# PEER expert stage: 112 candidate sums in place of 256, one-hot products on VectorE alone, four U blocks in flight, work between transpose and subtraction

## The reference, cut to what matters

```python
s = jnp.einsum('thpc,hpnc->thpn', q, keys32)
sv, si = lax.top_k(s, PEER_TOPK)                                   # 16 of 128 in each half
cand = (sv[:, :, 0, :, None] + sv[:, :, 1, None, :]).reshape(..., 256)
cidx = (si[:, :, 0, :, None] * N_SUBKEYS + si[:, :, 1, None, :]).reshape(..., 256)
cs, ci = lax.top_k(cand, PEER_TOPK)                                # 16 of the 256 sums
eidx = jnp.take_along_axis(cidx, ci, axis=-1)
g = jax.nn.softmax(cs, axis=-1)
act = jax.nn.gelu(jnp.einsum('thkd,td->thk', U[eidx], xb))
out = jnp.einsum('thk,thkd->td', g * act, V[eidx])
```

## Time and profile before

| what | value |
|---|---|
| time, median of 3 runs | 3904.52 us (3902.64 to 3905.26) |
| profiled execution: its time / its span | 3908.76 us / 3907.0 us |
| PE, DVE, ACT, POOL busy over the span | 87%, 76%, 27%, 29% |
| mean granted TensorE clock | 0.926 |
| moved from and to HBM | 822.80 MB, 211 GB/s |

### The profile page before, as it was taken

One profiled execution on the slowest core, in us unless ns is written; L12 is line 12 of the kernel. 1 busy time (PEld: TensorE's weight loads), 2 busy tenths in 40 slices (PEclk: granted clock), 3 DMA queues, 4 the chain that ended last, 5 costly groups with the idle time before them and its releaser, 6 DMA issues. The chain is left out here.

```text
span 3907.0 us, 52941 instructions
## 1 busy us (share of the span) xinstructions
PE 3384.6 (87%) x17880; PEld 3084.6 (79%) x17880; DVE 2964.2 (76%) x4958; ACT 1063.2 (27%) x1419; POOL 1152.0 (29%) x892
## 2 busy tenths in 40 slices
PE   6997558799799999888888886757999999999978
PEld 6996446699699999888888876756888888888878
DVE  3112773488788887999999987766999899999953
ACT  3213342211122222434343421112222222222233
POOL 0000000000000001666666766652333334333300
PEclk9998668899899999999999988888999999999989
DMA  3223211111234333888888899998999999999821
GB/s 105 91 91 103 78 49 50 27 39 36 77 100 135 99 98 109 278 275 278 276 287 280 281 302 327 314 330 301 355 356 355 340 355 356 355 359 354 297 77 49
DMA packets 411348, 822.80 MB, mean 211 GB/s; under 512 B 40704, under 2 KB 262800, under 8 KB 403856
## 3 DMA queue, kind: packets, MB, share of 16 engines
q1 hardware_dynamic: 300688, 419.27, 32.7%
q0 software_dynamic: 110592, 402.70, 30.2%
HBM read 696.74 MB, written 125.12 MB: 210 GB/s over the span
## 5 line engine op out<-in xcount | busy, mean ns | idle before, releaser
L232 PE MATMUL ea_pa<-rest_hi,ea_uhi 128*128 128x384 f32 x2048 | 738.2, 360 | 166.7 <-DVE ea_ulo L1428 166.7
L233 PE MATMUL ea_pa<-rest_lo,ea_uhi 128*128 128x384 f32 x2048 | 721.7, 352 | 0.0
L234 PE MATMUL ea_pa<-rest_hi,ea_ulo 128*128 128x384 f32 x2048 | 721.2, 352 | 0.0
L1136 POOL DMA_INDIRECT h<-in_peer_u,ga_rows x384 | 547.7, 1426 | 515.7 <-DVE ea_acc L1530 182.1
L1136 POOL DMA_INDIRECT eo_ring<-in_peer_v,ga_rows x384 | 405.4, 1056 | 660.0 <-DVE h L1799 632.1
L232 PEld LDWEIGHTS ea_pa<-rest_hi,ea_uhi 128*128 128x128 f32 x2048 | 416.3, 203 | 179.9 <-ACT ea_stage L1360 139.9
L1530 DVE CUSTOM_DVE_ANT_0 h<-h,plain 128x1024 f32<-128x1024 f32 x384 | 502.8, 1349 | 61.8 <-DMA h<-in_peer_u,ga_rows 61.7
L1799 DVE SCALAR_TENSOR_TENSOR h<-eo_ring,eo_share,h 128x1024 f32<-128x1024 f32 x384 | 490.8, 1279 | 0.7 <-DMA eo_ring<-in_peer_v,ga_rows 0.7
L233 PEld LDWEIGHTS ea_pa<-rest_lo,ea_uhi 128*128 128x128 f32 x2048 | 414.4, 202 | 0.0
L234 PEld LDWEIGHTS ea_pa<-rest_hi,ea_ulo 128*128 128x128 f32 x2048 | 412.3, 201 | 0.0
L1735 ACT ACTIVATE eo_phi<-eo_prod 128x512 fp32r<-128x512 f32 x192 | 121.6, 633 | 763.9 <-DVE eo_prod L1773 729.4
(11 more groups left out here) (313 smaller groups left out, 6669.9 us busy)
## 6 DMA issues: line engine op xcount, KB each, us to landing
ea_raw<-in_peer_u SPq DMA_DIRECT2D x512, 128.0 KB, 4.0
region<-in_peer_v SPq DMA_DIRECT2D x128, 512.0 KB, 11.0
act_scratch<-ea_stage SPq DMA_DIRECT2D x128, 384.0 KB, 3.2
w_scratch<-region SPq DMA_DIRECT2D x24, 2048.0 KB, 9.1
region<-w_scratch SPq DMA_DIRECT2D x16, 1536.0 KB
region<-act_scratch SPq DMA_DIRECT2D x16, 1536.0 KB
eo_wt<-w_scratch SPq DMA_DIRECT2D x16, 1536.0 KB, 13.2
eo_at<-act_scratch SPq DMA_DIRECT2D x16, 1536.0 KB, 17.4
```

What stands on the lines that cost most here:

```text
L232: nc.tensor.matmul(out, w[0], x[0], start=first, stop=False)
L233: nc.tensor.matmul(out, w[0], x[1], start=False, stop=False)
L234: return nc.tensor.matmul(out, w[1], x[0], start=False, stop=last)
L1136: nc.gpsimd.indirect_dma_start(out=dst, out_offset=None, in_=table, in_offset=bass.IndirectOffsetOnAxis(ap=self.rows[:, m % GT, m // GT:m ...
```

## The change

- `best_sums` adds only 4 x 16 sums (first four places of half 0 with all of half 1) and 12 x 4 (the rest of half 0 with the first four of half 1): 112 per head. The searches run over 112 elements. Splitting a place into its two indices then takes four more small instructions.
- `subkey` works in float16, laid out with four picks innermost: compare, multiply, three halving adds and a last add, where there was a compare, a multiply and a reduction in float32. The half's key numbers are spread to that layout by a copy in `best_sums`.
- POOL has no multiplication any more; DVE does both products of a batch (L1539 and L1540 after). POOL's program in the U stage is fetches alone.
- `raw` has four buffers, and SP loads four blocks ahead. Two halves of a pair become four places of a "quad".
- In stage A, DVE does `turn`, then the tile's picks work and dots, then `lo` (`split` with `beside`, and `dense_picks`). A gathered tile now has four blocks beside it, a dense tile eight, so stage A takes 3 x 4 + 6 x 8 = 60 blocks, where it took 54. Each dense tile's eight blocks also get 12 dots (72 in all).
- Stage W keeps its 24 groups, 48 blocks and 216 dots. Stage C keeps 16 blocks with 6 dots each (96 dots), where it had 24 blocks with 7 (168 dots). The last two blocks follow without dots. The loads and stores of the last blocks stand behind the first loads for the V stage (`after.first`) earlier by four blocks.

```diff
-        raw = sb("raw", [128, 2, 4, D // QR])
+        raw = sb("raw", [128, 4, 4, D // QR])
...
-        cand = region[:, 4608:6656].rearrange("p (h a b) -> p h a b", a=K, b=K)
-        eq = region[:, 6656:8704].rearrange("p (n a) -> p n a", a=K)
+        cand = region[:, 4608:4608 + PH * CANDS].rearrange("p (h c) -> p h c", c=CANDS)
+        eq = region[:, 5632:6656].bitcast(F16).rearrange("p (n x) -> p n x", x=K * QUAD)
+        sub = region[:, 6656:7168].bitcast(F16).rearrange("p (n x) -> p n x", x=K * QUAD)
...
-                    nc.gpsimd.tensor_tensor(hot[:, 2, b % 2], hot[:, 3, b % 2],
-                                            over_n(cur[:, n % 2, 3, c * BATCH:(c + 1) * BATCH]),
-                                            ALU.mult).then_inc(scaled_lo, 1)
...
+                def quad(q):
+                    for r in range(4):
+                        load(*at_block(q, r + 5))
+                        store(*at_block(q, r + 1))
...
-                    o.did(v_.tensor_tensor(cand, over_k(sv4[:, :, 0, :]), over_a(sv4[:, :, 1, :]), ALU.add))
-                    o.did(v_.tensor_copy(sif[:], one(si)))
+                    first = [128, PH, NARROW, K]
+                    o.did(v_.tensor_tensor(
+                        cand[:, :, 0:WIDE].rearrange("p h (a b) -> p h a b", b=K),
...
+                    rest = [128, PH, K - NARROW, NARROW]
...
+                    o.did(v_.tensor_copy(
+                        sub.rearrange("p n (k t) -> p (n k) t", t=QUAD),
...
-                    o.did(v_.tensor_single_scalar(ab[:, 1], places, K - 1, ALU.bitwise_and))
+                    o.did(v_.tensor_single_scalar(shifts[:, 0], places, 4, ALU.logical_shift_right))
+                    o.did(v_.tensor_single_scalar(shifts[:, 1], places, 2, ALU.logical_shift_right))
+                    o.settle()
+                    o.did(v_.scalar_tensor_tensor(out=ab[:, 0], in0=shifts[:, 1], scalar=float(NARROW - K),
+                                                  in1=shifts[:, 0], op0=ALU.add, op1=ALU.max))
...
+                    for half in (K * QUAD // 2, K * QUAD // 4, K * QUAD // 8):
+                        o.settle()
+                        o.did(v_.tensor_tensor(eq[:, :, 0:half], eq[:, :, 0:half], eq[:, :, half:2 * half], ALU.add))
                     o.settle()
-                    o.did(v_.tensor_reduce(rows[:, x], eq, AX.X, ALU.add))
+                    o.did(v_.tensor_tensor(rows[:, x].rearrange("p (n t) -> p n t", t=QUAD),
+                                           eq[:, :, 0:QUAD], eq[:, :, QUAD:2 * QUAD], ALU.add))
...
                     v_.tensor_tensor(hot[:, 1, c % 2], hot[:, 3, c % 2], gh, ALU.mult).then_inc(scaled_hi, 1)
+                    v_.tensor_tensor(hot[:, 2, c % 2], hot[:, 3, c % 2], gl, ALU.mult).then_inc(scaled_lo, 1)
...
+                for i in range(GT):
+                    split(*at_block(i, 2), lambda: next_sums(first, i))
+                    split(*at_block(i, 3), lambda: subkey(first, 0))
+                    split(*at_block(i, 4), lambda: subkey(first, 1))
+                    split(*at_block(i, 5), lambda: keep_chosen(first, i))
                     best_sums(first, i + 1)
...
+                def dense_picks(o, i, more):
...
+                    steps = {0: lambda: next_sums(o, i + GT), 2: lambda: subkey(o, 0), 3: lambda: subkey(o, 1),
+                             4: lambda: softmax(o, i + GT).then_inc(rows_ready, 1)}
+                    if more:
+                        steps[6] = lambda: best_sums(o, i + (GT + 1))
+                    steps[7] = lambda: rest_of_g(i)
+                    start = 0
+                    for r in range(4 * Q_DENSE):
+                        turn(*at_block(i * Q_DENSE + GT, r + 2))
+                        if r in steps:
+                            steps[r]()
+                        start = dots(i, PER_A, 0, start, DOTS_STEP[r])
+                        lo(*at_block(i * Q_DENSE + GT, r + 2))
+                    keep_dots(i, PER_A, 0)
...
+                for q in range(W0 + Q_W, TAIL):
+                    for r in range(4):
+                        split(*at_block(q, r + 2), some_dots)
+                for r in range(2, 4):
+                    split(TAIL, r)
```

More of the change, by code:

```diff
@@ L1220, in experts @@
         pw = ctx.enter_context(nc.psum_tensor("ea_pw", [128, 2, QUAD, NK], F32))
-        u_in = [s(f"u_in{u}") for u in range(2)]
+        u_in = [s(f"u_in{r}") for r in range(4)]
         stored = [s(f"stored{u}") for u in range(2)]
@@ L1264, in _ @@
                 e.wait_ge(ga.h_out, 16)
-                def fetch(m):
-                    if m >= PICKS:
-                        return
+                for m in range(PICKS):
                     if m >= RING:
@@ L1271, in fetch @@
                     ga.fetch(nc, P.a["peer_u"][0], m, ring[m % RING], fetched[m % RING])
[L1273 to L1283, removed]
-                    nc.gpsimd.tensor_tensor(hot[:, 2, b % 2], hot[:, 3, b % 2],
-                                            over_n(cur[:, n % 2, 3, c * BATCH:(c + 1) * BATCH]),
-                                            ALU.mult).then_inc(scaled_lo, 1)
-                while m < PICKS:
-                    fetch(m)
-                    m += 1
             @block.sync
@@ new lines, in next_sums @@
+                    o.settle()
+                    o.did(v_.tensor_scalar(ab[:, 2], ab[:, 0], float(NARROW), float(NARROW * (K - NARROW)),
+                                           ALU.mult, ALU.add))
+                    o.settle()
+                    o.did(v_.scalar_tensor_tensor(out=ab[:, 1], in0=ab[:, 0], scalar=float(K), in1=ab[:, 2],
+                                                  op0=ALU.mult, op1=ALU.min))
+                    o.settle()
+                    o.did(v_.tensor_tensor(ab[:, 1], places, ab[:, 1], ALU.subtract))
@@ L1537, in _, with dots, keep_dots @@
                 v_.sem_inc(scaled_lo, 2)
-                def picks_of(o, i, last):
-                    turn_lo(i * 3 + 1, 0)
-                    next_sums(o, i)
-                    turn_lo(i * 3 + 1, 1)
-                    subkey(o, 0)
-                    turn_lo(i * 3 + 2, 0)
-                    subkey(o, 1)
-                    turn_lo(i * 3 + 2, 1)
-                    last()
-                    turn_lo(i * 3 + 3, 0)
+                def dots(n, per, first, start, counts):
+                    m = start
+                    for _ in range(counts):
+                        dot(m, m % RING, n * (per // RING) + (first + m) // RING, acc[:, m:m + 1])
+                        m += 1
+                    return m
+                def keep_dots(n, per, first):
+                    e.wait_ge(ga.dotted, n * per + (first + per))
+                    v_.tensor_copy(ga.dots[:, bass.ds(n * per + first, per)], acc[:, 0:per]).then_inc(ga.dots_ready, 1)
                 first = Order(e, self_ok)
@@ L1641, in _ @@
                     last.then_inc(rows_t, 1)
[L1642 to L1653 removed]
+                with e.Fori(0, Q_W) as i:
+                    for r in range(4):
+                        for n in range(ND_N):
+                            product(*at_block(i + W0, r + 1), n)
+                            weights(i * 2 + r // 2, (r % 2) * ND_N + n)
+                with e.Fori(W0 + Q_W, TAIL) as i:
+                    quad(i)
+                for r in range(1, 4):
+                    for n in range(ND_N):
+                        product(TAIL, r, n)
 def expert_outputs(P, ga, loads):
```

287 lines of the change are left out of this document (137 added, 150 removed).

## The result

The changed kernel takes 3686.7 us (median of four runs, 3685.2 to 3689.9), the kernel before 3904.9 us in the same comparison: ratio 0.944, 95% interval 0.943 to 0.946. That is 218 us less, where 161 were predicted, and 13 us under the low end of the range. The profiled execution after has a span of 3683.9 us.

A forecast was written before the change was run, and what follows sets the result against it. It took PE to bound stage A, DVE stage W and DMA bytes (323 GB/s) stage C. Its terms, +44 - 93 - 112 = -161 us from 3908.76, gave 3748, against the median 3744 us; range 3700 to 3810.

The forecast's parts named there:

- Stage A, +44: Stage A: 60 blocks for 54 and a new PE stop make it 44 us longer, bounds +20 and +75.
- 6 x 6.8: Stage A: PE's stop and slow clock, with later `next_sums`, add 6.8 us to each of six dense tiles.
- The picks' terms: Stage A, DVE: `best_sums` 12.4 to about 8 us, `next_sums` 6.5 to 5.4, `subkey` 6.85 to about 4.2.
- 3 x 34.8 + 6 x 73.4: Stage A: three gathered tiles at 34.8 us and six dense tiles at 73.4 us, about 545 to 550 us.
- The products: Stage W: without POOL's products DVE is no longer held, and its products cost 0.63 to 0.71 us; fetches cost nothing.
- 7.9 - 2.6: Stage W, DVE per group: 7.9 us of holds by POOL's products go, four more products add 2.6 us.
- Stage W, -93: Stage W: 24 groups at 27.5 us, 660 us for 753, so 93 us less; bounds -129 and -57.
- the 27.5 us per group: Stage W: time taken between the 26.7 us DMA floor and 29 us with one DVE wait for a fetch per group.
- DMA gives more than stage C shows: Rival, stage W: it runs at DVE's 26.1 us per group, -129 us, 3708 us in all; chance 0.15.
- Stage C, -112: Stage C and tail: bound by bytes, 69 MB at 323 GB/s plus 28 us, 241 us for 353; bounds -100 and -122.
- Four blocks in flight: Stage A: the loads four blocks ahead are covered, 13.5 MB in 73 us, 185 GB/s.
- The V stage, 0: V stage: untouched, starting as before from the reload of `h` that waits for the last store; 0 us.

The follow-up runs named there:

- no_stop: The changed kernel with `rest_of_g` behind a dense tile's last subtraction and `next_sums` moved from its first to its second block: 3646.1 us.
- before_order: The kernel before with only its picks work and dots moved between a block's transpose and subtraction, in stages A and C: 3892.1 us.
- w_more_bytes: The changed kernel with half of each store of weights in stage W done a second time, to a scratch: 3723.3 us.
- two_ahead: The changed kernel with two buffers of U for four: 3853.7 us.
- before_dve_product: The kernel before with one edit alone, both products on DVE: 3878.2 us.
- best18: no_stop with 18 dots in each dense tile for 12, leaving 60 for stage C: 3598.9 us.
- best18_late_first: best18 with the first loads for V put behind the last loads of U on SP: 3594.5 us.

## Why the prediction was right in kind and wrong in size

- **Stage A, +44:** right in its mechanism, and closer in size than its terms. Stage A ends 46 us later (first copy of the next stage at 1590.9 for 1545.2). The stop of 3.74 us with slow clock behind it is the one worked out, and no_stop shows its price: 41 us in all, where the sum had 6 x 6.8. A dense tile takes 73.3 us (PE's transposes of the picks, from 1220.3 for the first of six tiles to 1587.0 for the last), forecast 73.4. The picks' terms hold too: behind the boundary shown, `next_sums` takes 5.3 us (5.4 forecast), a `subkey` 4.3 (4.2), its float16 compare 1.18 (1.2). But 3 x 34.8 + 6 x 73.4 is 545, and 538 less one stop, where the text has 545 to 550 and +44 stands for 551. The last 8 to 15 us of the agreement are luck.
- **The products:** right. No hold is left (0.69 us for 2.154), the fetches cost the products and dots nothing, and DVE's busy time in stage W fell from 30.4 us per group to 24.9, by 5.5 us where 7.9 - 2.6 were forecast. The Trainium skill's "SBUF — State Buffer", section "Who interferes with whom", says that a DVE instruction with two SBUF inputs contends with a GpSimd instruction that reads SBUF, and not with one that only writes it. The products agree, 2.77 us beside GpSimd's product and 0.69 us without; no run shows which of the two kinds a fetch is, only that 216 of them leave the products undisturbed.
- **Stage W, -93: this step failed.** "At stage C's 323 GB/s that is 26.7 us", and the 27.5 us per group built on it, took the rate of one stage for the limit of the DMA engines, because its share stood at 0.98. Measured, the stage fell by 134 us (744 to 610). before_order shows that rate to follow DVE's order, w_more_bytes shows 350 GB/s in stage W itself, 359 behind its start. A higher rate stands in the same trace, in its V stage, where PE is busy throughout, so that 354 GB/s need not be the limit either:

```profile
2750.00:3600.00 850.00, 849.43 (x3741) 701.76 (x3740) 785.89 (x899) 200.44 (x261) 330.39 (x313) 1.00 1.00 354
```

  At 354 GB/s the DMA floor would have been 8.63 MB / 354 = 24.4 us, under DVE's 26.1, and the stage DVE's. That is the rival "DMA gives more than stage C shows" (0.15, 3708 us), which is what happened in stage W; its total is 21 us too high, since it left stage C at the old rate. A smaller error stood beside it: the stretch taken for stage W, 753 us, was 9 us longer than the stage (744 us, 31.0 us per group), so DVE's floor was 25.7. It came out as 25.4.
- **Stage C, -112:** the term was mis-sized by the same rate. 69 MB at 354 GB/s are 195 us, with the tail of 28 us 223; measured 228, forecast 241 (-125 for -112). Put together, the forecast's stage A, 24 x 25.7 us and 223 us end the U stage at 1589 + 617 + 223 = 2429 us; the last gelu ended at 2427, with 7 us less in stage W and 5 more in stage C cancelling.
- **The Trainium skill's bandwidth.** The prediction named 425 GB/s, from the Trainium skill's "DMA: Bandwidth & Descriptors", section "Bandwidth". No run here comes near it over 200 us: the highest is 365 (w_more_bytes, 1750 to 1950). The section "Specifications" of that page of the Trainium skill gives some 358 GB/s as the limit of a core's memory, and the rows come within 2% of that (354 in the V stage, 356 in stage C, 359 and 365 in w_more_bytes).
- **Four blocks in flight** were costed at nothing, since 185 GB/s is little. The cost of their absence was not asked: 167 us in this schedule, 102 of them by the order on SP. As the change has them, the sum was not hurt. But with two blocks and the same order on SP the other parts together are worth 50 us (two_ahead, 3853.7 for 3903.9), and the product's move alone 26 (before_dve_product).
- **The V stage, 0:** right (1256.6 for 1257.8 us).

## What to carry to other kernels

A DMA share near 1 is no proof of a limit: look for the highest rate that any stage of the same trace keeps up, and take a lower one for a bound only when no engine's waits or order can explain it. A faster engine needs its input sooner, so price each part of a change with the others taken away: here the product's move, the four buffers and the narrower search are worth 133, 167 and 60 us together with the others, and the first alone 26. A wait can move on by one block instead of going, so ask what stands behind the waiting instruction before moving it.

## What was not expected of the hardware

- The DMA share says little of the rate: 0.98 at 325 GB/s, 0.99 at 332, 1.00 at 350 and at 354, 1.02 at 359, 1.04 at 356.
- The issue of one 1.5 MB load held SP's queue for 16.8 us in best18, and the next load of U was issued only at its end; in best18_late_first the issue of the same load took 6.5 us.
